# A normalisation border in which the next phase's first chunk runs on unscaled x, with reordered pair ends, in a three-block transformer kernel

## The chip, the core and the metric

One core of a Trainium2 chip. The metric is the time of one execution on the device in microseconds; several runs of one kernel agree within 0.1%. TensorE (PE) does matmuls and loads weights (PEld), VectorE (DVE) and ScalarE (ACT) do elementwise work, GpSimd (POOL) does elementwise work here, SyncE (SP) issues the weight loads.

## The reference, cut to what matters

512 tokens of width 1024, float32, pass three blocks: a gated linear recurrence with stick-breaking attention ("even"), a matrix-memory mixer with gates ("odd"), each followed by a convolutional gated MLP, and a block of dilated attention and latent sparse attention followed by a gated MLP. Every sub-block begins with

```
h   = rmsnorm(x, g) * (1 + scale) + shift      # scale, shift: from the condition vector, one value per channel
mod = silu(c) @ ada_w + ada_b                  # gives shift, scale, gate for each sub-block
x   = x + gate * sub_block(h)
rmsnorm(x, g) = x * rsqrt(mean(x * x, -1) + 1e-6) * g
```

and the output is a last rmsnorm of x. So between two sub-blocks stands a border: the last residual must be in x before the mean of squares of any token is known, and every input of the next matmul carries 1/rms.

## The kernel before, in words

**Layout.** x lies in SBUF with channels on partitions: `X` is 8 tiles (k = 0 to 7) of 128 channels by 512 tokens. Weights come as 302 chunks of 128x1024 float32 in one stream (`wstream`). A chunk of a "tile" phase holds the 8 k tiles for 128 output channels. Products are done in three passes of a rounded format: high x high, high x low, low x high, so each operand is split into a high half (`w_hi`, `h_hi`) and a low half (`w_lo`, `h_lo`). One chunk is 8 x 3 = 24 matmuls of 512 columns into one PSUM bank `gemm0` to `gemm3` (L477 to L479).

**The weight stream.** SyncE loads chunk n into one of 2 raw slots. GpSimd (`split_at`, L432 on) waits until TensorE has finished chunk n-4, does a tiny gate instruction (L439), writes the high half (L440) and subtracts for the low half (L442), into one of 4 slots. `w_split` counts chunks ready, `pe_done` chunks finished.

**Residual phases.** `even_out`, `odd_out` and `attn_out` have 8 chunks of 8 k tiles; `down0` to `down2` have 8 times three chunks with 22 k tiles. Chunk m of the output gives channel tile m. VectorE, when `pe_done` says so, adds gate x bank to `X[m]` (`residual`, L1234); ScalarE squares it (L2085); VectorE adds the square to `sq_acc` (`add_square_prev`, L1511). The last tile is done in two halves (`last_residual`, L1241; squares L2098). VectorE does residual m, then the addition for m, then residual m+1, in this order.

**The border** (`norm`, on each engine). TensorE sums `sq_acc` and the last square over partitions (L581), ScalarE takes the root (L1890), VectorE the reciprocal (L1267), TensorE spreads 1/rms over the partitions (`token_rows`, L608). VectorE then scales tile k (`scaled`, L1281: X x gain x 1/rms), ScalarE adds the shift and rounds (`high_tiles`, L1906), VectorE gives the low half (`low`, L1288), k by k. TensorE fills its waits with matmuls on constants (`keep_warm`, L574). The next phase starts with `first_tiles` (L533, L534, L518): two chunks at once, k by k, as tiles become ready, in an order written by hand; then chunk by chunk. Borders r = 1, 2, 3, 5 stand in front of `ffn0`, `odd_in`, `ffn1` and `ffn2`; "first", "second", "third" and "fourth border" below mean these.

**The odd mixer's pair end.** Heads go in pairs g = 0 to 3. VectorE makes the weights of a head (`mweights`, L1641, L1645), sums them over blocks (`mweight_sum`, L1652 to L1655), copies the inverse norms as a high and low pair (`pair_copy`, L1666, L1667). TensorE multiplies values (`mvalues`, L950), sums squares and denominators (`msums`: L955, L959), spreads inverse norms (`minv_spread`, L983) and starts `odd_out` with three chunks at once, between whose k steps stand `turn_sums` (L989) and other small steps.

**Attention's pairs.** For p = 0 to 7 TensorE turns the exponentials (`turn`, pieces c = 0 to 4, L1156), spreads inverse sums (L1167, piece 5), multiplies values (L1182), and does the scores of pair p+2 (L1133) between pieces 1 and 2. ScalarE does the exponentials (L2307) and copies each turned piece out of PSUM (L2318, L2320, L2325); VectorE adds biases (L1804, L1808), takes maxima with the logits (`logits`, L1821), and normalises the output (L1838, L1842). A piece may be turned only when the copy two pieces back is done.

## Time and profile before

| what | value |
|---|---|
| median of 3 runs | 1936.18 us (1935.46 to 1936.76) |
| the profiled execution | 1939.17 us |
| its span, first to last instruction | 1937.4 us |
| mean granted clock of TensorE | 0.993 |
| busy: PE, DVE, ACT, POOL | 98%, 53%, 23%, 62% |
| chain that ended last | PE 92%, DVE 5%, ACT 2%, DMA 1% |

The chain is the work that ended last, followed back from the end. The granted clock is a share of TensorE's full speed (2.4 GHz); 0.50 is the lower level (1.2 GHz). In a timeline each line gives the start in us from the span's start, the length in us, the engine, the line of the kernel, the operation, output <- inputs, the shape and how many instructions are merged; in brackets stands the idle time of the engine before it and what ended it. A matmul is listed with its full latency (0.39 us) while the next starts 0.23 us after it.

### The profile page before, as it was taken

How to read it: one execution, taken by the hardware profiler on the slowest of the kernel's cores; microseconds unless marked ns; L12 is line 12 of the kernel's file. 1: busy time of each engine (PE TensorE's matmuls, PEld its weight loads, DVE VectorE, ACT ScalarE, POOL GpSimd, SP SyncE). 2: the span in 40 equal slices, each digit the busy share in tenths (PEclk: the TensorE clock that was granted, in tenths of full speed). 3: DMA queues.
4: the chain of work that ended last, by engine and by line, in shares of the span. 5: the costliest groups of instructions: out<-in, count | busy, mean ns of one | idle time of the engine just before them, and what ended most of it. 6: DMA issues, size and time to landing. Idle time of an engine off the chain costs nothing.

```text
span 1937.4 us, 25522 instructions
## 1 busy us (share of the span) xinstructions
PE 1906.3 (98%) x8976; PEld 1541.9 (80%) x8976; DVE 1033.7 (53%) x1518; ACT 441.9 (23%) x774; POOL 1197.1 (62%) x915
## 2 busy tenths in 40 slices
PE   8999999999999999999999999999999999999998
PEld 5888868888888887767888888887776788888887
DVE  4565357666655554586666563243888443232222
ACT  4211342211110022342211111022239221111000
POOL 3844315888777956434688887755551456666673
PEclk9999999999999999999999999999999999999999
DMA  8522223555554432211455553332220122322332
GB/s 339 178 99 95 94 83 109 195 195 195 195 195 176 172 100 83 75 55 55 163 195 195 195 184 120 108 109 87 66 87 1 49 83 97 97 97 97 99 108 76
DMA packets 67665, 242.26 MB, mean 125 GB/s; under 512 B 7658, under 2 KB 8170, under 8 KB 67602
## 3 DMA queue, kind: packets, MB, share of 16 engines
q1 hardware_dynamic: 65536, 237.01, 35.6%
q10 hardware_dynamic: 2066, 4.38, 0.7%
q8 instruction: 44, 0.72, 0.2%
q14 instruction: 19, 0.16, 0.0%
HBM read 239.26 MB, written 2.10 MB: 125 GB/s over the span
## 4 chain that ended last, share of the span: by engine, by line
PE 92%; DVE 5%; ACT 2%; DMA 1%; issue 0%; ACTq 0%; DVEq 0%
PE gemm L477 23%; PE gemm L479 23%; PE gemm L478 23%; PE gemm L533 2%; PE gemm L534 2%; PE gemm L504 2%; PE gemm L505 2%; PE gemm L506 2%; PE gemm L518 2%; PE mix L770 1%; DVE sq_acc L1511 1%; PE gemm L1182 1%; PE mix L608 1%; PE gemm L1156 1%; PE mix L574 1%; PE mix L1133 1%
## 5 line engine op out<-in xcount | busy, mean ns | idle before, releaser
L442 POOL TENSOR_TENSOR w_lo<-w_raw,w_hi 128x1024 fp32r<-128x1024 f32 x302 | 741.5, 2455 | 25.2
L477 PE MATMUL gemm<-h_hi,w_hi 128*128 128x512 f32 x1464 | 571.7, 391 | 0.0
L479 PE MATMUL gemm<-h_hi,w_lo 128*128 128x512 f32 x1464 | 569.8, 389 | 0.0
L478 PE MATMUL gemm<-h_lo,w_hi 128*128 128x512 f32 x1464 | 569.6, 389 | 0.0
L439 POOL TENSOR_TENSOR pool_gate<-pool_gate 128x1 f32<-128x1 f32 x298 | 116.5, 391 | 602.4 <-PE gemm L479 337.6
L440 POOL TENSOR_SCALAR w_hi<-w_raw 128x1024 fp32r<-128x1024 f32 x302 | 341.0, 1129 | 26.8 <-DMA w_raw<-wstream 26.8
L479 PEld LDWEIGHTS gemm<-h_hi,w_lo 128*128 128x128 f32 x1464 | 274.8, 188 | 57.1
L478 PEld LDWEIGHTS gemm<-h_lo,w_hi 128*128 128x128 f32 x1464 | 274.9, 188 | 57.0
L477 PEld LDWEIGHTS gemm<-h_hi,w_hi 128*128 128x128 f32 x1464 | 274.9, 188 | 56.9
L1216 DVE CUSTOM_DVE_ANT_0 ada_raw<-ada_raw,c_act 128x1024 f32<-128x1024 f32 x128 | 224.8, 1772 | 100.4 <-DMA ada_raw<-adastream 100.4
L479 PE MATMUL gemm<-p_hi,w_lo 128*128 128x512 f32 x528 | 205.4, 389 | 0.0
L477 PE MATMUL gemm<-p_hi,w_hi 128*128 128x512 f32 x528 | 205.4, 389 | 0.0
L478 PE MATMUL gemm<-p_lo,w_hi 128*128 128x512 f32 x528 | 205.4, 389 | 0.0
L1234 DVE SCALAR_TENSOR_TENSOR x_res<-gemm,modv,x_res 128x512 f32<-128x512 f32 x42 | 31.4, 747 | 204.8 <-PE gemm L479 190.7
L1539 DVE TENSOR_TENSOR work<-work,gemm 128x512 f32<-128x512 f32 x66 | 45.4, 688 | 177.8 <-PE gemm L479 140.4
L1541 DVE TENSOR_TENSOR p_lo<-work,p_hi 128x512 f32 x66 | 89.9, 1362 | 61.4 <-ACT p_hi L2123 61.4
L1511 DVE TENSOR_TENSOR sq_acc<-sq_acc,sq_tile 128x512 f32<-128x512 f32 x42 | 104.7, 2494 | 29.4 <-ACT sq_tile L2085 29.4
L477 PEld LDWEIGHTS gemm<-p_hi,w_hi 128*128 128x128 f32 x528 | 99.1, 188 | 20.7
L478 PEld LDWEIGHTS gemm<-p_lo,w_hi 128*128 128x128 f32 x528 | 99.1, 188 | 20.6
L479 PEld LDWEIGHTS gemm<-p_hi,w_lo 128*128 128x128 f32 x528 | 99.1, 188 | 20.4
L2085 ACT ACTIVATE sq_tile<-x_res 128x512 f32<-128x512 f32 x42 | 26.6, 633 | 378.0 <-DVE x_res L1234 378.0
L2117 ACT ACTIVATE work<-work 128x512 f32<-128x512 f32 x44 | 27.8, 633 | 308.5 <-DVE work L1534 308.5
(376 smaller groups left out, 2216.5 us busy)
## 6 DMA issues: line engine op xcount, KB each, us to landing
w_raw<-wstream SPq DMA_DIRECT2D x302, 512.0 KB, 3.5
ada_raw<-adastream SPq DMA_DIRECT2D x128, 512.0 KB, 4.3
a_early<-adastream SPq DMA_DIRECT2D x8, 1024.0 KB, 18.6
out<-x_res SPq DMA_DIRECT2D x8, 256.0 KB, 2.2
x_res<-x_in SPq DMA_DIRECT2D x2, 512.0 KB, 5.1
x_res<-x_in ACTq DMA_DIRECT2D x2, 512.0 KB, 7.7
c_act<-c_in ACTq DMA_DIRECT2D x2, 512.0 KB, 5.9
b_dist<-const_in ACTq DMA_DIRECT2D x1, 512.0 KB
```

Source lines behind the costliest of these rows:

```text
L439: pool.tensor_tensor(pgate[:], pgate[:], pgate[:], ALU.mult)
L440: pool.tensor_scalar(whi[s][:], raw[:, u % RAW, :], 1.0, 0.0, ALU.mult, ALU.add).then_inc(w_hi_done, 1)
L442: pool.tensor_tensor(wlo[s][:], raw[:, u % RAW, :], whi[s][:].bitcast(F32), ALU.subtract).then_inc(w_split, 1)
L477: pe.matmul(out_ap, w_h, r_h, start=first, stop=False)
L478: pe.matmul(out_ap, w_h, r_l, start=False, stop=False)
L479: return pe.matmul(out_ap, w_l, r_h, start=False, stop=last)
L504: pe.matmul(G[j][:], a, wh, start=(k == 0), stop=False)
L505: pe.matmul(G[j][:], a, wl, start=False, stop=False)
L1216: dve.tensor_tensor_reduce(w, w, c, 1.0, start, ALU.mult, ALU.add, total).then_inc(ada_used, 1)
L1511: dve.tensor_tensor(sqacc[:], sqacc[:], sqt[:, m % 2, :], ALU.add).then_inc(sq_added, 1)
L1539: dve.tensor_tensor(work[:, 2 + jj, :], y, G[2 * jj + 1][:], ALU.mult).then_inc(gfree[2 * jj + 1], 1)
L1541: dve.tensor_tensor(Plo[:, ds(2 * i + jj, 1), :].rearrange("p a t -> p (a t)"), work[:, 2 + jj, :], Phi[:, ds(2 * i + jj, 1), :].rearrange ...
```

## The change

At borders r = 1, 2, 3, 5 the next phase's chunk 0 is multiplied with u = X x gain, without 1/rms and without the shift. ScalarE makes u's high half for each tile as its residual comes in (ahead of the square), VectorE the low half (`unscaled_low`). VectorE further adds the two halves of chunk 0's weights (`whole_weights`) and forms the products of weights and shift, summed over k (`shift_products`, 8 instructions, each waiting for the one before); TensorE sums these over partitions into one column. TensorE runs chunk 0 between the border's own small matmuls (`norm_beside`), in place of the constant matmuls; VectorE multiplies the full bank by 1/rms and adds the column (`scale_first_chunk`). The normalised tiles are made as before, now without the first tile's halves, and `first_tiles` runs chunks 1 to 3 together.

Apart from the borders: at the odd mixer's pair end the last two weight sums, `gated(6)`, the pair copy, the spreads and the square sums stand in another order. In the attention the last two scores of a pair come between pieces 3 and 4; the logits take their blocks in the order 3, 1, 2, 0; VectorE copies five turned pieces of pairs 6 and 7 in ScalarE's place, and turn 0 of pair 7 stands ahead of the values of pair 6.

```diff
+NEXT = {1: ("ffn0", 1, 24, 32), 2: ("odd_in", 2, 48, 56), 3: ("ffn1", 3, 72, 80), 5: ("ffn2", 6, 120, 128)}
+VECTOR_PIECES = [(6, 2), (6, 3), (6, 4), (7, 1), (7, 3)]
...
@@ TensorE
-            def first_tiles(phase, fill, count=2, before={}):
+            def first_tiles(phase, fill, count=2, before={}, begin=0):
...
-                if done == 0 and phase in FILL:
+                if done == 0 and phase in [nxt[0] for nxt in NEXT.values()]:
+                    first_tiles(phase, FILL[phase], 3, begin=1)
+                    first = 1
+                elif done == 0 and phase in FILL:
...
+            def norm_beside(r):
...
+                pe.wait_ge(w_split, n + 1)
+                pe.wait_ge(gfree[0], G0[phase][0])
+                chunk_tiles((0, 1))
+                pe.wait_ge(sq_added, KT * r + KT - 1)
+                partial_sums(0, sqacc, True, False)
+                pe.wait_ge(sq_ready, KT * (r + 1))
+                partial_sums(0, sqt[:, 1, :], False, True).then_inc(norm_sum, 1)
+                chunk_tiles((2, 3))
+                bc[0] += 1
+                pe.wait_ge(rstd_ready, bc[0])
+                pe.matmul(M[0][:, 0:1], shift_sums, const("ones")[:, 0:1], start=True, stop=True)
+                token_rows(rstdps, 0).then_inc(rstd_bc, 1)
+                chunk_tiles((4, 5, 6, 7)).then_inc(pe_done, 1)
...
@@ TensorE, odd pair end (g == 3), after mvalues(6)
+            pe.wait_ge(sig("msq"), 6)
+            pe.wait_ge(sig("mabs"), 1)
+            msquares(5)
+            mvalues(7)
+            minv_spread(0)
+            minv_spread(1)
+            pe.wait_ge(sig("mwsum"), 7)
+            pe.wait_ge(sig("msq"), 7)
+            msquares(6)
+            mdenominator(6)
+            minv_spread(2)
+            minv_spread(3)
             pe.wait_ge(sig("mnum"), 8)
+            def last_squares():
+                minv_spread(4)
...
+                mdenominator(7)
+                msquares(7)
...
@@ TensorE, attention
-                turn(p, (0, 1))
+                turn(p, (0, 1) if p < 7 else (1,))
                 if p + 2 < 8:
-                    scores(p + 2)
-                turn(p, (2, 3, 4))
+                    scores(p + 2, SCORE_ORDER[:6])
+                turn(p, (2, 3))
+                if p + 2 < 8:
+                    scores(p + 2, SCORE_ORDER[6:])
+                turn(p, (4,))
                 inverse_rows(p)
+                if p == 6:
+                    turn(7, (0,))
                 values(p)
...
@@ VectorE, borders
+            def unscaled_low(r, k):
+                uhi, ulo = unscaled(r)
+                dve.scalar_tensor_tensor(out=ulo[:, k, :], in0=X[:, k, :], scalar=norm_gain(r)[:, k:k + 1], in1=uhi[:, k, :].bitcast(F32),
+                                         op0=ALU.mult, op1=ALU.subtract).then_inc(sig("u_tiles"), 1)
...
+                link(dve.tensor_tensor(both, whi[n % SPL][:].bitcast(F32), wlo[n % SPL][:].bitcast(F32), ALU.add))
...
+                link(dve.tensor_scalar(shift_sums, both[:, 0:P], modv[:, shift:shift + 1], None, ALU.mult))
+                for k in range(1, KT):
+                    link(dve.scalar_tensor_tensor(out=shift_sums, in0=both[:, k * P:(k + 1) * P], scalar=modv[:, shift + k:shift + k + 1],
+                                                  in1=shift_sums, op0=ALU.mult, op1=ALU.add))
...
+            def scale_first_chunk(phase):
+                dve.wait_ge(pe_done, N0[phase] + 1)
+                link(dve.tensor_copy(shift_bias, M[0][:, 0:1]))
+                link(dve.tensor_copy(sqacc[:], rstdps[:]))
+                link(dve.tensor_tensor(G[0][:], G[0][:], sqacc[:], ALU.mult))
+                link(dve.tensor_scalar(G[0][:], G[0][:], shift_bias, None, ALU.add))
...
@@ VectorE, residual_tiles (even_out, odd_out, attn_out)
                     residual(N0[phase] + m, m, m % 4, gate)
                     add_square_prev(r, m)
+                    unscaled_low(r, m)
+                    if m == KT - 4:
+                        whole_weights(r)
+                    if m == KT - 3:
+                        shift_products(r)
                 last_residual(N0[phase] + KT - 1, KT - 1, 3, gate)
...
@@ VectorE, down
+                            if r in NEXT:
+                                unscaled_low(r, 4 * i + m)
+                                if 4 * i + m == KT - 2:
+                                    whole_weights(r)
+                                    shift_products(r)
...
@@ VectorE, odd pair end: mweights(7) first, then
+            pair_copy(GIR, GM[0:EARLY_HEADS, :], EARLY_HEADS)
+            mweight_sum(6)
             normed_head(0)
             normed_head(1)
             split_head(0)
+            mweight_sum(7)
             split_head(1)
             normed_head(2)
+            gated(6)
             normed_head(3)
...
@@ VectorE, attention
+                if p == 7:
+                    copy_piece(7, 1)
+                    copy_piece(7, 3)
                 if p >= 1:
                     pair_low(p - 1)
+                if p == 6:
+                    for c in (2, 3, 4):
+                        copy_piece(6, c)
...
@@ ScalarE, squares
                     act.wait_ge(gfree[m % 4], m // 4 + G0[phase][m % 4] + 1)
+                    if r in NEXT:
+                        act.activation(unscaled(r)[0][:, m, :], X[:, m, :], ACT.Identity, scale=norm_gain(r)[:, m:m + 1])
                     act.wait_ge(sq_added, KT * r + m - 1)
```

## Rows read from the trace of the kernel before

**Rows 1.** The page, part 1: busy time and share of the span of each engine
```profile
PE 1906.3 (98%) x8976; PEld 1541.9 (80%) x8976; DVE 1033.7 (53%) x1518; ACT 441.9 (23%) x774; POOL 1197.1 (62%) x915
```
**Rows 2.** PE's waits (us, times, longest); its timeline (start, us) at attention's end
```profile
PE gemm L1156 <- ACT b_pt L2320: 5.7, 8, 2.0
...
1498.21 1.09 PE L1156 MATMUL gemm<-cst,ada_raw 128*128 128x128 f32 x8
...
1502.86 1.08 PE L1156 MATMUL gemm<-cst,ada_raw 128*128 128x128 f32 x4 [2.02 <-ACT b_pt L2320]
...
1516.25 0.50 PE L533 MATMUL gemm<-h_hi,w_hi 128*128 128x512 f32 x1
```
**Rows 3.** Timeline of PE at the odd mixer's pair end
```profile
869.83 0.73 PE L983 MATMUL mix<-o_gi_hilo,o_sel 40*128 40x512 f32 x2 [2.52 <-DVE o_gi_hilo L1667]
870.48 4.12 PE L950 MATMUL gemm<-o_w,o_v 128*128 128x512 f32 x8
...
881.37 0.44 PE L989 MATMUL mix<-cst,o_gm 40*128 40x40 f32 x4
```
**Rows 4.** Timeline of PE at the first border
```profile
321.68 0.95 PE L581 MATMUL mix<-cst,sq_acc 128*128 128x1 f32 x8
...
327.61 0.47 PE L533 MATMUL gemm<-h_hi,w_hi 128*128 128x512 f32 x1
```
**Rows 5.** Timeline of DVE, then PE, over odd_out and the third border
```profile
896.20 0.75 DVE L1234 SCALAR_TENSOR_TENSOR x_res<-gemm,modv,x_res 128x512 f32<-128x512 f32 x1 [2.56 <-PE gemm L518]
...
900.32 0.74 DVE L1234 SCALAR_TENSOR_TENSOR x_res<-gemm,modv,x_res 128x512 f32<-128x512 f32 x1
...
924.87 0.86 DVE L1241 SCALAR_TENSOR_TENSOR x_res<-gemm,modv,x_res 128x256 f32<-128x256 f32 x2
...
923.13 0.39 PE L478 MATMUL gemm<-h_lo,w_hi 128*128 128x512 f32 x1
923.36 0.39 PE L479 MATMUL gemm<-h_hi,w_lo 128*128 128x512 f32 x1
...
931.01 0.47 PE L533 MATMUL gemm<-h_hi,w_hi 128*128 128x512 f32 x1
```
**Rows 6.** Timeline of DVE at the first border
```profile
317.88 2.83 DVE L1511 TENSOR_TENSOR sq_acc<-sq_acc,sq_tile 128x512 f32<-128x512 f32 x1 [0.70 <-ACT sq_tile L2085]
321.88 0.88 DVE L1241 SCALAR_TENSOR_TENSOR x_res<-gemm,modv,x_res 128x256 f32<-128x256 f32 x2 [1.17 <-PE gemm L479]
```
**Rows 7.** Timeline of POOL at the first border
```profile
317.76 2.40 POOL L442 TENSOR_TENSOR w_lo<-w_raw,w_hi 128x1024 fp32r<-128x1024 f32 x1
```
**Rows 8.** Timeline of all engines, cut to POOL and linked DVE instructions
```profile
752.65 1.21 DVE L1602 TENSOR_TENSOR_SCAN o_gb<-o_gm,o_gf 8x512 f32<-8x512 f32 x1
...
753.82 1.05 POOL L440 TENSOR_SCALAR w_hi<-w_raw 128x1024 fp32r<-128x1024 f32 x1
753.89 1.50 DVE L1603 TENSOR_TENSOR o_ga<-o_gi,o_gb 8x512 f32<-8x512 f32 x1
754.95 2.71 POOL L442 TENSOR_TENSOR w_lo<-w_raw,w_hi 128x1024 fp32r<-128x1024 f32 x1
755.43 3.30 DVE L1605 TENSOR_TENSOR_SCAN o_gm<-o_ga 8x512 f32<-8x512 f32 x1
```
**Rows 9.** A group by line (busy, mean ns), then L1808 and L1227 alone (ns min/median/max)
```profile
L1906 ACT ACTIVATE h_hi<-work,modv 128x512 fp32r<-128x512 f32 x35 | 25.4, 725 | 18.7 <-DVE work L1281 17.9
...
L1808 DVE SCALAR_TENSOR_TENSOR b_bias<-b_dist,b_score x32: 279/483/684, 1463.6 to 1492.8; 128x128 f32<-128x128 f32 x8, 128x256 f32<-128x256 f32 x8, 128x384 f32<-128x384 f32 x8, 128x512 f32<-128x512 f32 x8
...
L1227 DVE TENSOR_TENSOR modv<-mod_sums,cols x32: 161/924/2235, 60.9 to 1171.0; 128x4 f32 x22, 128x4 f32<-128x4 f32 x10
```
**Rows 10.** Timeline of POOL ahead of the second border (down0 to odd_in)
```profile
675.14 2.39 POOL L442 TENSOR_TENSOR w_lo<-w_raw,w_hi 128x1024 fp32r<-128x1024 f32 x1
...
687.09 0.19 POOL L439 TENSOR_TENSOR pool_gate<-pool_gate 128x1 f32<-128x1 f32 x1 [0.48 <-PE gemm L479]
```
**Rows 11.** Stretches: us, PE, PEld, DVE, ACT, POOL busy (x), PEclk, DMA share, GB/s
```profile
1504.00:1508.00 4.00, 4.00 (x24) 2.37 (x26) 0.00 (x0) 1.17 (x2) 0.00 (x0) 0.50 0.01 4
```

More of the change, by code:

```diff
@@ L85, with copies_by_scalar, copies_by_vector @@
 BANK_J = [(1, 384), (2, 0), (1, 0), (0, 0)]
+def copies_by_scalar(p, c):
+    return sum(6 * q + d <= 6 * p + c and (q, d) not in VECTOR_PIECES for q in range(8) for d in range(6))
+def copies_by_vector(p, c):
+    return sum(6 * q + d <= 6 * p + c for q, d in VECTOR_PIECES)
 def slopes():
@@ L1895, in norm @@
                     act.preload_act_table(table)
-                high_tiles(shift)
+                for k in range(KT):
+                    if k == 4:
+                        act.wait_ge(pe_done, N0[NEXT[r][0]] + 1)
+                    act.wait_ge(t_ready, scaled[0] + k + 1)
+                    act.activation(Hhi[:, k, :], work[:, k % 4, :], ACT.Identity, bias=modv[:, shift + k:shift + k + 1]).then_inc(hhi_ready, 1)
+                scaled[0] += KT
+                act.wait_ge(h_ready, KT * (fill + 1))
             def high_tiles(shift):
-                act.wait_ge(t_half, borders[0])
+                act.wait_ge(t_half, 1)
                 act.activation(Hhi[:, 0, 0:HALF], work[:, 0, 0:HALF], ACT.Identity, bias=modv[:, shift:shift + 1])
```

184 lines of the change are left out of this document (123 added, 61 removed).

## The prediction, made before the change was run

> **What bounds the kernel now.** I read the page first. TensorE is busy for 98% of the span [rows 1], so time can only go where it issues something that isn't needed, waits, or runs at its lower clock. The waits of PE add up to little: 5.7 us behind ScalarE's copies of turned weights [rows 2], 2.5 us at the odd mixer's end [rows 3], and 1.3 us at the third border. The rest of what can be had is at the norm borders. At the first, the last useful matmul makes room at 321.68 and the next phase starts at 327.61 [rows 4]: 5.93 us of sums, spread and warming matmuls. The second border and the fourth repeat this within 0.15 us. The third takes 931.01 - 923.59 = 7.42 us (923.36 and one matmul pitch, 923.36 - 923.13 = 0.23) [rows 5], since its last residual is 1.3 us late.
>
> The second thing to see is how VectorE and GpSimd take turns. The addition of squares at 317.88 took 2.83 us, and ended 0.5 us after GpSimd's 317.76 + 2.40 [rows 6, 7]: only the last 0.5 was its own. Residuals, which read PSUM, keep to 0.75 in the same stretches [rows 5]. So a VectorE instruction with two SBUF inputs waits for the GpSimd instruction that runs, and GpSimd waits for it. When both are behind, one chunk's residual, square and addition and one weight split go round in 900.32 - 896.20 = 4.1 us [rows 5]. Three VectorE instructions linked by semaphores show what a chain does while GpSimd has work: L1602 ended, GpSimd's 753.82 took the turn, L1603 stood 1.50 us, GpSimd's 754.95 took the next, and L1605 stood 3.30 us instead of about 1.2 [rows 8]. Even a 128x4 addition costs 0.92 us in the median against 0.16 at least [rows 9].
>
> **The change, part by part.** *Borders, what TensorE does.* One chunk is 24 matmuls, 5.44 us. It moves into the border; warming matmuls go. With nobody late, TensorE needs, from its last matmul: k 0,1 1.36; sums 0.8 and 0.8; k 2,3 1.36; the shift column and four row spreads 1.15 (12 records took 1.34, so 8 take 0.9, and 0.25 for the column); k 4 to 7 2.72: 8.2 us. Before, border and chunk were 5.93 + 5.44 = 11.37. That is 3.2 us saved a border, and the most there is. The square root (0.26) and reciprocal lie under k 2,3. ScalarE's new wait for this chunk ahead of tile 4 costs nothing, tile 4 being due 3 us after it is done even then; no DMA is moved, and SyncE's weight loads wait for splits as before. Afterwards three chunks share each k step, 9 x 0.227 = 2.04 us, against VectorE's 1.32 a step, so by k = 6 it is 4.3 us ahead, which covers the four instructions on the full bank (about 2.3 us by four instructions like the 0.6 to 0.75 ones; 2.3 us a border if the cover were gone). GpSimd's next splits come one at a time, 3.6 us each, under 5.44: nothing.
>
> *Borders, what VectorE and ScalarE get.* For each of seven residuals ScalarE gets one more activation, ahead of the square (0.72, 0.62 after overlap) [rows 9]: the addition is ready 2.07 us after the residual instead of 1.45, which GpSimd's 2.40 hides. VectorE gets a subtraction with two SBUF inputs, 0.6: the round grows from 4.1 to 4.7. Against 5.44 a chunk it still catches up, by 0.74 instead of 1.34. Once come the sum of the weight halves and eight linked products of 128 columns: such an instruction takes 0.28 for 128 columns and 0.68 for 512 [rows 9], so the sum over 1024 takes 1.2, a product 0.28, 0.31 with the link, all eight 2.5 us if nothing came between. They stand ahead of residual 6, and that ahead of the last one, so whatever they wait, the norm waits.
>
> *First border, step by step.* The pair was done six chunks before the last, at 321.67 - 32.7 = 289.0. Residual 4 starts at 289.1 + 4 x 4.7 = 307.9; its addition ends 311.7, the subtraction 312.35. GpSimd's waiting first half-split takes the turn to 313.4, the weight sum runs to 314.5, GpSimd's second to 316.85, addition 5 to 317.35, subtraction to 318.0. Then GpSimd to 319.1, product 1, GpSimd to 321.6, product 2. TensorE's last matmul at 321.67 has freed another slot, so GpSimd goes again, to 323.0 and, after product 3, to 325.5; products 4 to 8 end at 327.0. Residual 6, two activations, addition at 329.1, subtraction, and the last residual starts at 330.2, not 321.88 [rows 6]. From there: squares 1.45, sums 0.8, 1.36, 1.15, 2.72 = 7.5, so the three chunks start at 337.7. Before, the same point was 327.61 + 5.44 = 333.05: **+4.6 us**. TensorE stands from 323.0 to 329.7 meanwhile. The fourth border has the same rhythm: **+4.6**.
>
> *Third border.* Three chunks finish together at 896, so the round of 4.7 never catches up: the last residual starts at about 937.3 instead of 924.87 [rows 5], the three chunks at 944.7 against 931.01 + 5.44 = 936.45: **+8.2**.
>
> *Second border.* A chunk of down0 takes 15 us and nobody is late, but the weight sum waits for the split that ends at 677.5 [rows 10], and the eight products then meet three more splits, the last released by the last matmul (687.09 [rows 10]). By the same walk they end at 691.2 and the last residual is 4.2 us late: **+0.5**. Two turns fewer and it is -3.2; I take +0.5, because the last two products fall on that last split.
>
> *The clock.* After a wait of 2.02 us the attention's end ran at a granted 0.50, the lower of the two levels (1.2 GHz) [rows 2, 11], until its values ended at about 1509, some 6.6 us. Waits of 6 us and more at each of three borders should do the same. Bounds: nothing, to half of 6.6, 3.3 each; I take 2 each, since part of the work there waits for others anyway: **+6**. The Trainium skill (TensorE: Matmul & The Clock Gate, "Why this matters for your kernels") warns against letting TensorE stand between bursts; by that rule all three borders lose, as in this term, and taking out the warming matmuls is wrong wherever something else is late.
>
> *Odd pair end.* TensorE's wait of 2.5 us and the eight matmuls that took 4.12 us, at half clock [rows 3, 11], instead of 2.3, come from VectorE's weight sum and pair copy ahead of them. Putting both behind the last weights lets the last values run at 867.5 instead of 870.48; what is put off returns as waits of 0.4, 0.2 and 1.3 us (a spread that needs the third normed head). I get 879.4 for what stood at 881.37 [rows 3]: **-2** (0 to -4).
>
> *Attention.* Six of the eight waits for a copy are short: 5.7 less 2.02 and some 1.7 leaves 0.34 us each [rows 2]; two scores put there fill it, but ScalarE's copy can come only 0.1 to 0.3 earlier: five pairs, -1.2. At the end 1498.21 to 1516.25 is 18.0 us [rows 2]; with VectorE copying five pieces (0.69 each, like its other reads of a bank) turn 4 of pair 6 starts at 1501.2, not 1502.86, its values at 1503.4 at full clock, and the last values end at 1511.9: -4.3. Together **-5.5** (-2 to -8).
>
> **Sum.** 4.6 + 0.5 + 8.2 + 4.6 + 6 - 2 - 5.5 = +16.4 us. The profiled execution took 1939.17 us (span 1937.4), 3.0 above the median of 1936.18, so the sum is put on the median: 1952.6.
>
> **The rivals.** *Chain in one piece.* The products go through without GpSimd between them. The Trainium skill (VectorE: DVE Perf Modes, "The DRAIN you can't avoid") reports that semaphores between VectorE instructions cost nothing extra; by that rule the chain is as long linked as not. The mechanism here: 2.5 us in one stretch. The last residual is then 3.5 us late at borders one and four (-0.3 each), on time at the second (-3.2), 8.5 late at the third (+3.4, and 2 of clock): +1.6 - 7.5, 1930. The linked three [rows 8] speak against it, with three instructions out of three giving way; four unlinked ones were not all interrupted.
> *No holding at all.* The new instructions overlap GpSimd. The borders reach 8.2 us, only the third keeps 0.5 of lateness: -9.1 - 7.5 = -16.6, 1919.6. Subtractions of the same form stood 2 us behind GpSimd elsewhere, so this needs a trace wrong about three kinds of instruction; a luckier order of splits would come near it.
> *Pair ends bring nothing.* The waits move to the third head's spread and the copies; the borders as forecast: 1960.
> The sign turns on where the last residual starts: late by less than about 4 us, a border gains; by more, it loses.
>
> **How the numbers follow.** Forecast 0.66 (own range 1942 to 1962: the clock term from 0 to 10, the second border from -3.2, the ends from -3 to -11), one piece 0.17, no holding 0.12, no gain at the ends 0.05. The range 1928 to 1961 leaves out no holding and the top of the last. About 0.2% (3.9 us) is what a measurement can tell from none. Faster: no holding and most of one piece, 0.26; same, the rest of it and the forecast's lowest edge, 0.08; slower 0.66.
>
> **What would show it.** In the changed kernel's timeline: GpSimd's half-splits between the products at borders one, three and four; products at 0.28 with stands of 1.1 and 2.4 among them; the last residual 8 us (third border: 13) after the phase's last matmul; a wait of PE for the addition of squares of 6 to 12 us in three places, and a granted clock of 0.50 after it. At the two pair ends, a continuous PE. I am wrong if those residuals start within 1 us, or if the chunk beside the norm is done before the root.

## The result, and the profile after

The changed kernel took **1968.9 us** in the median of four runs (1965.12 to 1973.89) beside 1936.47 for the kernel before: a ratio of **1.016, interval 1.0144 to 1.0177**. Slower, as forecast, but above the range of 1928 to 1961. The profiled execution was the fastest of the four, 1965.12 us with a span of 1963.2; that of before, 1939.17, was longer than all four of its runs. So the two traces are 26.0 us apart where the medians are 32.4; the accounts below are made between the traces, and what separates them from the medians comes up with the experiments. One execution of experiment 10 was in a slow state (2736 us at a granted clock of 0.65) and is left out of its ratio.

First the page, part 1, and then the largest waits of PE (us in total, times, longest) of the changed kernel:

```profile
PE 1904.3 (97%) x8920; PEld 1539.6 (78%) x8920; DVE 1098.5 (56%) x1603; ACT 456.2 (23%) x797; POOL 1220.6 (62%) x915
```

```profile
PE mix L608 <- DVE sq_acc L1657: 23.7, 3, 11.3
PE mix L608 <- ACT sq_tile L2282: 6.4, 1, 6.4
...
PE gemm L500 <- DVE work L1680: 2.5, 2, 1.3
...
PE gemm L1229 <- ACT b_pt L2505: 1.5, 1, 1.5
```

Beside [rows 1], TensorE has 56 instructions fewer and is busy for 2 us less, yet the span grew by 26. The first two rows are the four borders: 30.1 us of waits where there was 1.3. The last row is the attention's end, 1.5 us instead of the 5.7 of [rows 2].

VectorE at the first border, with the columns start, us, engine, line, operation, tiles; a bracket is the idle time ahead and what ended it. Then GpSimd in the same stretch, then TensorE:

```profile
312.14 2.06 DVE L1368 TENSOR_TENSOR work<-w_hi,w_lo 128x1024 f32<-128x1024 f32 x1
...
317.59 1.07 DVE L1373 TENSOR_SCALAR work<-work,modv 128x128 f32<-128x128 f32 x1
318.70 7.68 DVE L1375 SCALAR_TENSOR_TENSOR work<-work,modv 128x128 f32<-128x128 f32 x7
326.42 0.75 DVE L1314 SCALAR_TENSOR_TENSOR x_res<-gemm,modv,x_res 128x512 f32<-128x512 f32 x1
...
329.75 0.87 DVE L1321 SCALAR_TENSOR_TENSOR x_res<-gemm,modv,x_res 128x256 f32<-128x256 f32 x2
```

```profile
318.66 2.39 POOL L465 TENSOR_TENSOR w_lo<-w_raw,w_hi 128x1024 fp32r<-128x1024 f32 x1
321.80 0.22 POOL L462 TENSOR_TENSOR pool_gate<-pool_gate 128x1 f32<-128x1 f32 x1 [0.75 <-PE gemm L502]
321.99 1.05 POOL L463 TENSOR_SCALAR w_hi<-w_raw 128x1024 fp32r<-128x1024 f32 x1
323.12 2.34 POOL L465 TENSOR_TENSOR w_lo<-w_raw,w_hi 128x1024 fp32r<-128x1024 f32 x1
```

```profile
321.26 0.39 PE L502 MATMUL gemm<-h_hi,w_lo 128*128 128x512 f32 x1
...
329.22 1.87 PE L608 MATMUL mix<-cst,sq_acc 128*128 128x1 f32 x8 [6.21 <-DVE sq_acc L1657]
...
331.12 1.87 PE L608 MATMUL mix<-cst,sq_tile 128*128 128x1 f32 x8
332.85 0.77 PE L500 MATMUL gemm<-p_hi,w_hi 128*128 128x512 f32 x1
...
340.29 0.39 PE L556 MATMUL gemm<-h_hi,w_hi 128*128 128x512 f32 x1
```

The seven products of L1375 took 7.68 us. One by one their durations are 2.50, 0.35, 0.35, 1.17, 2.40, 0.35 and 0.35: each long one ends within 0.15 us after a GpSimd instruction (318.66 + 2.39, 321.99 + 1.05, 323.12 + 2.34), and where GpSimd stands a product takes 0.35. The last residual starts at 329.75, 8.3 us after the phase's last matmul (321.26 and one pitch, 321.49), and the three chunks start at 340.29.

Then the clock. Stretches of the changed kernel: from and to, length, busy time of PE, PEld, DVE, ACT, POOL, then PEclk:

```profile
322.00:327.00 5.00, 1.01 (x5) 0.51 (x3) 4.85 (x5) 0.00 (x0) 3.38 (x3) 1.00 0.67 220
328.00:337.00 9.00, 7.75 (x29) 7.08 (x30) 2.96 (x6) 3.35 (x6) 0.00 (x0) 0.50 0.19 79
338.00:341.00 3.00, 3.00 (x15) 2.45 (x14) 2.87 (x5) 1.68 (x3) 0.46 (x2) 1.00 0.00 0
700.00:709.00 9.00, 4.70 (x16) 4.12 (x17) 4.51 (x7) 2.91 (x5) 1.97 (x1) 0.50 0.44 144
942.00:958.00 16.00, 9.07 (x34) 8.31 (x35) 7.99 (x14) 4.15 (x7) 2.34 (x1) 0.50 0.35 129
1584.00:1593.00 9.00, 6.19 (x22) 5.62 (x23) 3.68 (x7) 4.15 (x7) 0.00 (x0) 0.50 0.18 60
```

TensorE had stood since 322.85 when the clock fell at about 327, and it did not come back until after the sums, two k steps and most of the spread: all four borders run the first half of their critical matmuls at 1.2 GHz, and k 4 to 7 again at 2.4 GHz. Eight sums take 1.87 us instead of 0.95 [rows 4].

An account of the two traces, by landmarks of TensorE. A border is the time from the phase's last matmul to the next phase's three chunks (before: its start plus one chunk of 5.44 us):

| stretch | before | after | difference | forecast |
|---|---|---|---|---|
| border 1 | 11.37 | 18.80 | +7.4 | +4.6 and 2 of clock |
| ffn0 | 234.04 | 235.49 | +1.45 | 0 |
| border 2 | 11.51 | 17.28 | +5.8 | +0.5 |
| odd mixer to its last matmul | 225.31 | 223.12 | -2.2 | -2 |
| border 3 | 12.86 | 24.64 | +11.8 | +8.2 and 2 |
| index and attention phases | 217.80 | 212.76 | -5.0 | -5.5 |
| border 4 | 11.38 | 18.06 | +6.7 | +4.6 and 2 |

The sum is 25.9, for spans 25.8 apart. Two differences are not in the table, since they cancel. ffn1 took 1.5 us more, as ffn0 did. And at the border ahead of the index phase (r = 4), which the change leaves alone, the kernel before took 8.3 us from the last matmul to the next phase (1290.17 to 1298.44) and the changed kernel 6.8 (1315.90 to 1322.69): before's trace has a granted clock of 0.50 there from 1294.0 to 1297.5, the other has 1.00. Six of the fourteen traces of this case have that stretch (before and experiments 5 to 8 and 10), so it is not the change that takes it away, and it hides ffn1's loss.

### The profile page after: what moved, and what is told of

It reads as the page before. It is cut to its first block, busy times and chain, and to the rows that moved or that the text cites. A ratio compares the mean times of both kernels' runs of the same rounds, so it can differ in the third digit from the quotient of the medians.

```text
span 1963.2 us, 25500 instructions
## 1 busy us (share of the span) xinstructions
PE 1904.3 (97%) x8920; PEld 1539.6 (78%) x8920; DVE 1098.5 (56%) x1603; ACT 456.2 (23%) x797; POOL 1220.6 (62%) x915
## 4 chain that ended last, share of the span: by engine, by line
PE 75%; issue 8%; DVE 6%; POOL 6%; DMA 3%; ACT 1%; SPq 0%; POOLq 0%; DVEq 0%; ACTq 0%
PE gemm L500 19%; PE gemm L502 19%; PE gemm L501 19%; POOL w_lo L465 3%; POOL w_hi L463 2%; DMA w_raw<-wstream 2%; PE gemm L527 2%; PE gemm L528 2%; PE gemm L529 2%; PE mix L828 1%; DVE work L1375 1%; PE gemm L1257 1%; PE gemm L1229 1%; PE mix L1199 1%; PE mix L500 1%
## 5 line engine op out<-in xcount | busy, mean ns | idle before, releaser
L500 PE MATMUL gemm<-h_hi,w_hi 128*128 128x512 f32 x1408 | 551.1, 391 | 2.6 <-DVE work L1680 2.5
L502 PE MATMUL gemm<-h_hi,w_lo 128*128 128x512 f32 x1408 | 548.5, 390 | 0.0
L501 PE MATMUL gemm<-h_lo,w_hi 128*128 128x512 f32 x1408 | 548.4, 389 | 0.0
L463 POOL TENSOR_SCALAR w_hi<-w_raw 128x1024 fp32r<-128x1024 f32 x302 | 361.6, 1197 | 26.8 <-DMA w_raw<-wstream 26.8
L500 PE MATMUL gemm<-p_hi,w_hi 128*128 128x512 f32 x552 | 217.3, 394 | 0.0
L501 PE MATMUL gemm<-p_lo,w_hi 128*128 128x512 f32 x552 | 216.4, 392 | 0.0
L502 PE MATMUL gemm<-p_hi,w_lo 128*128 128x512 f32 x552 | 216.4, 392 | 0.0
L1687 DVE TENSOR_TENSOR p_lo<-work,p_hi 128x512 f32 x66 | 104.8, 1588 | 61.4 <-ACT p_hi L2309 61.4
L1657 DVE TENSOR_TENSOR sq_acc<-sq_acc,sq_tile 128x512 f32<-128x512 f32 x42 | 80.2, 1909 | 46.6 <-ACT sq_tile L2269 46.6
L2309 ACT ACTIVATE p_hi<-work 128x512 f32 x66 | 41.7, 632 | 155.2 <-DVE work L1685 155.2
## 6 DMA issues: line engine op xcount, KB each, us to landing
a_early<-adastream SPq DMA_DIRECT2D x8, 1024.0 KB, 18.6
```

The source lines that it names most:

```text
L463: pool.tensor_scalar(whi[s][:], raw[:, u % RAW, :], 1.0, 0.0, ALU.mult, ALU.add).then_inc(w_hi_done, 1)
L500: pe.matmul(out_ap, w_h, r_h, start=first, stop=False)
L501: pe.matmul(out_ap, w_h, r_l, start=False, stop=False)
L502: return pe.matmul(out_ap, w_l, r_h, start=False, stop=last)
L1657: dve.tensor_tensor(sqacc[:], sqacc[:], sqt[:, m % 2, :], ALU.add).then_inc(sq_added, 1)
L1687: dve.tensor_tensor(Plo[:, ds(2 * i + jj, 1), :].rearrange("p a t -> p (a t)"), work[:, 2 + jj, :], Phi[:, ds(2 * i + jj, 1), :].rearrange ...
```

## The experiments

Twelve kernels ran, each beside the kernel before on the same chip. Over all these runs the kernel before had a median of 1938.4 us (1935.18 to 1945.36, 35 runs). That is a spread of 0.5%, where three runs had given 0.1%: a difference of 1 or 2 us between two medians is not resolved here.

**1. The pair ends alone.** The kernel before with the new odd pair end and the new attention, no border work.

```diff
 for g in range(4):
     mweights(2 * g)
-    mweight_sum(2 * g)
+    if g < 3:
+        mweight_sum(2 * g)
...
-            scores(p + 2)
-        turn(p, (2, 3, 4))
+            scores(p + 2, SCORE_ORDER[:6])
+        turn(p, (2, 3))
+        if p + 2 < 8:
+            scores(p + 2, SCORE_ORDER[6:])
+        turn(p, (4,))
```

> The kernel before with the two pair ends of the change and none of its border work. Theory (the parts add up): by the landmarks of the two traces the odd mixer from the second border to the third is 3.96 - 1.82 = 2.1 us shorter with the change and the attention phase 5.0 us shorter, so 1936.5 - 7.1 = 1929.4 us, 1928 to 1931. Rival (the ends gain only because the borders ahead of them left GpSimd less behind): the same ends give less than 3 us here, 1934 or more.

Measured: 1933.85 us, ratio 0.998 (0.997 to 0.9991), 4.1 us less than its kernel before, between theory and rival. Its trace, of an execution of 1936.66 us and so above that median, gives a reason. The odd mixer's last matmul comes 2.6 us earlier and the attention phase is 5.1 us shorter, both as the theory has it. But from the third border's last matmul to the next phase's start it took 10.7 us (923.99 to 934.70) instead of 7.4 [rows 5]. Stretches of this run, and of the kernel with the attention part alone (experiment 12), where nothing ahead of the third border is changed:

```profile
926.40:933.00 6.60, 6.60 (x26) 6.06 (x26) 0.67 (x3) 2.23 (x4) 2.34 (x1) 0.50 0.84 304
```

```profile
925.60:932.20 6.60, 6.60 (x26) 6.06 (x27) 0.82 (x3) 2.25 (x5) 2.50 (x2) 0.50 0.82 289
```

The old third border has a 1.3 us wait, and in some runs half clock follows it, at 3.3 us (in experiment 11 for 3.5 us only, at 1.5), and in some not (the kernel before). With one trace for each kernel, that this is chance and not the changed code is argued, not shown.

**2. The borders alone.** The kernel before with the border work, old ends.

```diff
-            norm(1, 2, col("norm_ffn_g", 0, 8), (24, 32))
+            norm_beside(1, 2)
...
+                    if m == KT - 4:
+                        whole_weights(r)
+                    if m == KT - 3:
+                        shift_products(r)
```

> The kernel before with the border work alone, old pair ends. Theory: the borders and what follows them carry the whole loss, 7.4 + 5.7 + 11.8 + 6.7 at the four borders and 1.5 in the first feed-forward, 33 us by the landmarks of the traces: 1969 to 1976 us, last residual 8 us after the phase's last matmul at borders one and four, 7 at two, 13 at three. Rival (the new pair end puts the third border's VectorE behind, so a part of that loss belongs to the ends): the third border costs 5 us less here than the 11.8 of the change, 1964 or less.

Measured: 1974.88 us, ratio 1.0182 (1.016 to 1.0203), 37 us more than before. The borders took 19.6, 17.7, 24.2 and 18.7 us; the third cost 11.3 more than before's 12.86, so the rival, that the ends had a part in it, falls. The parts add up: -4.1 and +36.9 make +32.8, the whole change +32.4.

**3. Warming matmuls in the waits, first size.**

```diff
                 chunk_tiles((0, 1))
+                keep_warm({1: 54, 2: 2, 3: 96, 5: 54}[r])
                 pe.wait_ge(sq_added, KT * r + KT - 1)
                 partial_sums(0, sqacc, True, False)
+                keep_warm({1: 2, 2: 48, 3: 2, 5: 2}[r])
```

> The changed kernel with warming matmuls put into the time in which TensorE waits at the four borders, nothing else altered. Theory (the low clock is a cost of its own of 2.4 to 3.8 us a border, 11.6 in all: from the last residual to the three chunks it took 10.5, 10.0, 11.3 and 9.9 us against 7.5 worked out at full clock): no stretch at 0.50 at the borders, sums of 0.95 us for eight instead of 1.87, and 1968.9 - 11 = 1958 us, 1955 to 1961. Rival (the stretch behind the last residual is set by VectorE and ScalarE, the clock costs what was forecast or less): 1963 or more.

Measured: 2036.54 us, ratio 1.051 (1.0484 to 1.0536), far outside both ranges. The theory was not at fault but the size: I had taken one warming matmul as a single pass.

```profile
324.24 23.47 PE L601 MATMUL mix<-cst 128*128 128x256 f32 x108
...
347.54 0.95 PE L608 MATMUL mix<-cst,sq_acc 128*128 128x1 f32 x8
```

That is TensorE at the first border: 54 warming matmuls are 108 records of 0.217 us, 23.5 us where 6 were to be filled. But the sums that follow take 0.95. The kernel served to size the next.

**5. The same, sized: 13, 12, 26 and 13 matmuls in the long wait of each border, one in the short.**

```diff
+                keep_warm({1: 13, 2: 1, 3: 26, 5: 13}[r])
...
+                keep_warm({1: 1, 2: 12, 3: 1, 5: 1}[r])
```

> The changed kernel with warming matmuls in the waits of the four borders, now sized by the last run (54 of them took 23.5 us, 0.43 each): 13, 13, 26 and 13 of them for waits of 6.2, 6.4, 11.3 and 6.2 us. Theory (the lower clock costs 2.4 to 3.8 us a border): no stretch at 0.50 at the borders, the sums 0.95 us for eight, and 11 us less than the changed kernel's 1968.9, so 1958 us, 1955 to 1961. Rival (VectorE and ScalarE set the pace there, the clock costs what was forecast, 6 us, or less): 1963 or more.

Measured: 1958.83 us, ratio 1.0095 (1.0067 to 1.0123), 10 us less than the changed kernel: the theory's number. TensorE at the fourth border:

```profile
1580.18 5.77 PE L601 MATMUL mix<-cst 128*128 128x256 f32 x26
1586.63 1.05 PE L608 MATMUL mix<-cst,sq_acc 128*128 128x1 f32 x8 [0.67 <-DVE sq_acc L1659]
...
1588.52 1.05 PE L608 MATMUL mix<-cst,sq_tile 128*128 128x1 f32 x8 [0.30 <-ACT sq_tile L2284]
```

From the last residual to the three chunks it took 7.65 us at borders two and four (705.78 to 713.43, 1587.15 to 1594.80), against 10.0 and 9.9 in the changed kernel; 7.5 was the forecast's. At borders one and three it still was 9.2 and 9.3: short waits were left everywhere, and there a spell at 0.50 followed (335.3 to 338.7 at the first). Between the two traces the four borders are 7.8 us shorter, together. What remains is 20 us over the kernel before, with the lateness as it was: 8.3, 7.2, 13.4 and 8.3 us.

**4. The shift column on TensorE.** No weight sum and no products on VectorE; the same column from 16 one-column matmuls.

```diff
+                for k in range(KT):
+                    for w in (whi, wlo):
+                        pe.matmul(M[0][:, 0:1], w[s][:, k * P:(k + 1) * P].bitcast(F32), modv[:, shift + k:shift + k + 1],
+                                  start=(k == 0 and w is whi), stop=(k == KT - 1 and w is wlo))
...
-                    if m == KT - 4:
-                        whole_weights(r)
-                    if m == KT - 3:
-                        shift_products(r)
```

> The changed kernel without the weight sum and the eight linked products on VectorE: the column of shifts comes from 16 matmuls of one column (the high and the low half of the weights times the shift), put ahead of the sum of squares. Theory (those nine instructions, each giving GpSimd a turn, make the last residual late): it starts within 1 us of the phase's last matmul at borders one, two and four, and 5 to 6 us after it at the third, where the rounds of 4.6 us still do not catch up; 16 matmuls cost 1.9 us at 0.12 each; a border takes 9.9 us instead of 11.4, the third 13 to 16, so 1936.5 - 4.5 + 2 + 1.5 - 7.1 = 1928 us, 1925 to 1932. Rival A (the subtraction beside each residual is what makes it late): last residuals 4 us late and more at all borders, above 1945. Rival B (the small matmuls cost more than 0.2 us each on TensorE's path): lateness gone but 1933 to 1938.

Measured: 1951.19 us, ratio 1.0056 (1.0037 to 1.0075). The lateness is gone as the theory says: last residuals 0.20, 0.20, 5.0 and 0.20 us after the phase's last matmul. The subtraction of rival A is cleared, but for the 5.0 us of the third border. But the borders took 16.6, 15.0, 16.6 and 16.6 us, not 9.9, and rival B was too small as well. TensorE at the first border, and two stretches of it:

```profile
330.91 0.57 PE L651 MATMUL mix<-modv,w_hi 128*128 128x1 f32 x2
...
332.62 1.84 PE L608 MATMUL mix<-cst,sq_acc 128*128 128x1 f32 x8
334.33 1.85 PE L608 MATMUL mix<-cst,sq_tile 128*128 128x1 f32 x8
336.04 0.77 PE L500 MATMUL gemm<-p_hi,w_hi 128*128 128x512 f32 x1
```

```profile
326.96:330.80 3.84, 3.84 (x30) 3.61 (x29) 0.94 (x3) 1.36 (x3) 3.45 (x3) 1.00 0.80 273
331.00:341.00 10.00, 10.00 (x41) 9.32 (x41) 1.13 (x3) 1.55 (x2) 0.00 (x0) 0.50 0.30 106
```

Each of the 16 is two records, 0.22 us together, so 3.6 us at full clock. And though TensorE waited for nothing, its clock fell at 331, 2.6 us into the one-column matmuls, and the sums and k steps behind them ran at half: 4.3 us of column, 3.4 of sums. At the third and fourth border it fell at the same place; at the second the column ran at full clock (701.61 to 705.09) and the clock fell at 706.4, in the sums behind it. An engine can be busy for 100% of a stretch and still lose its clock, as here at all four borders.

**6. Two products instead of eight.**

```diff
-                link(dve.tensor_scalar(shift_sums, both[:, 0:P], modv[:, shift:shift + 1], None, ALU.mult))
-                for k in range(1, KT):
-                    link(dve.scalar_tensor_tensor(...))
+                whole = both.rearrange("p (k t) -> p k t", k=KT)
+                link(dve.tensor_tensor(whole, whole, modv[:, shift:shift + KT].unsqueeze(2).broadcast_to([P, KT, P]), ALU.mult))
+                link(dve.tensor_reduce(shift_sums, both.rearrange("p (k t) -> p t k", k=KT), axis=mybir.AxisListType.X, op=ALU.add))
```

> The changed kernel with the eight linked products as two instructions, one product over 1024 columns and one sum over the eight pieces. Theory (what costs is that each instruction waits for GpSimd's half-split in progress; fewer instructions, fewer stands): the two end 1.5 to 2 us earlier than the eight at each border, 1968.9 - 7 = 1962 us, 1959 to 1965. Rival (the length of the chain's own work is what counts, 2.6 us against 3.1): 1965 to 1969. A sum over strided pieces that takes over 3 us by itself would make it slower than 1969.

Measured: 1950.3 us, ratio 1.0058 (1.0036 to 1.0081), 18.6 us less than the eight: the theory's side, at more than twice its size. VectorE at the first border, then at the second:

```profile
318.19 2.06 DVE L1374 TENSOR_TENSOR work<-work,modv 128x1024 f32<-128x1024 f32 x1
320.29 2.04 DVE L1375 TENSOR_REDUCE work<-work 128x128 f32<-128x1024 f32 x1
322.36 0.75 DVE L1314 SCALAR_TENSOR_TENSOR x_res<-gemm,modv,x_res 128x512 f32<-128x512 f32 x1
...
327.24 0.86 DVE L1321 SCALAR_TENSOR_TENSOR x_res<-gemm,modv,x_res 128x256 f32<-128x256 f32 x2
```

```profile
688.13 1.23 DVE L1368 TENSOR_TENSOR work<-w_hi,w_lo 128x1024 f32<-128x1024 f32 x1 [3.57 <-POOL w_lo L465]
689.40 1.95 DVE L1374 TENSOR_TENSOR work<-work,modv 128x1024 f32<-128x1024 f32 x1
691.38 2.02 DVE L1375 TENSOR_REDUCE work<-work 128x128 f32<-128x1024 f32 x1
694.03 0.88 DVE L1321 SCALAR_TENSOR_TENSOR x_res<-gemm,modv,x_res 128x256 f32<-128x256 f32 x2 [0.63 <-PE gemm L502]
```

Two instructions of the same content take 4.1 us where eight took 8.8. The product stands once for GpSimd; the sum, with a single SBUF input, runs beside GpSimd's half-split (319.26 to 322.51) and takes no turn at all. At the second border they are done at 693.4, just before the phase's last matmul (693.77) frees the next slot: VectorE waits for TensorE again, the last residual is 0.3 us late, the border is 8.4 us instead of 17.3, and its clock is not lost. At the others the last residual is still 5.2, 10.3 and 5.2 us late. Borders: 16.0, 8.4, 20.4 and 15.0, together 19.0 us less. I had priced two turns, and neither the clock nor the turn that the last matmul releases. The Trainium skill (SBUF — State Buffer, "SBUF: two separate sides") calls the port pair of VectorE and GpSimd an exclusive lock, held for a whole instruction by whichever starts first; the rows of both kernels agree: the products' stands end where GpSimd's instruction ends.

**7. No products.** The nine instructions are left out and with them the first chunk's shift; the rest is the changed kernel.

> The changed kernel with the weight sum and the eight products left out (the first chunk's shift is missing from the output). Theory (they alone make the last residual late, and the 8.2 us of a border stand as worked out): last residual 0.2 us after the phase's last matmul at borders one, two and four, 5 at the third; 8.2 us from last matmul to the three chunks instead of 11.4, at the third 13 to 16 with its clock; 1938 - 9.6 + 3 + 1.5 - 4 (the pair ends as measured) = 1929 us, 1926 to 1932. Rival (the clock falls in any case once the warming matmuls are gone, since one-column matmuls do not hold it): 10.5 to 11 us at borders one, two and four, 1935 to 1938, and stretches at 0.50 at all four.

Measured: 1931.82 us, ratio 0.9961 (0.9948 to 0.9974), in the range. A stretch that is the whole first border:

```profile
321.76:330.16 8.40, 8.40 (x51) 7.41 (x50) 4.36 (x9) 4.29 (x7) 3.57 (x3) 1.00 0.70 248
```

TensorE never waits, the clock stays at 1.00 and the border takes 8.4 us, 0.2 over the 8.2 worked out. Borders two and four take 8.4 too. So the warming matmuls were not missed where nobody was late. The third took 15.6, with its residual 5.0 late and 6.8 us at 0.50. Against the changed kernel it is 37 us, the price of nine instructions at each of four borders, which take 4.0 us a border when nothing is in their way (1.2 for the sum, 8 x 0.35).

**8. The products later.** The weight sum behind the last residual, the products spread over the k steps of the three chunks, the column's matmul at the step k = 5. Nothing left out.

```diff
+                whole_weights(r)
+                products = iter(range(KT))
                 rms_n[0] += 1
                 ready(inverse_rms(4, rms_n[0]))
...
                 for k in range(KT):
+                    for _ in range((0, 1, 2, 2, 2, 1, 0, 0)[k]):
+                        shift_product(r, next(products))
```

> The changed kernel with its weight sum put behind the last residual and the eight products into the first k steps of the next phase's other three chunks, where VectorE has about 0.7 us a step to spare and GpSimd has no slot to fill; the column's matmul waits until the fifth step. Nothing is left out. Theory (same work, moved off the chain that sets the norm): the borders as without the products, plus 1 to 2 us at each where the weight sum meets a half-split ahead of the reciprocal: 1931 us, 1928 to 1936. Rival (VectorE loses its lead of 4.3 us in the three chunks and TensorE waits there for low tiles): waits of PE for h_lo of 2 us and more at each border, 1938 to 1945.

Measured: 1939.29 us, ratio 1.0003 (0.9992 to 1.0013): no difference from before. The time is in the rival's range (1938 to 1945) and above the theory's; the wait is another than the rival's, for the column and for banks and not for low tiles. The borders took 8.2, 8.2, 15.9 and 8.2 us. What they gained was asked back behind them. TensorE waited three times for the column (3.1 us together), ffn0 took 237.5 us instead of 234.0, and the odd mixer to its last matmul 226.4 where the changed kernel took 223.1: VectorE's lead was spent and it came late to the first groups of both.

**9. A version meant to beat both.** Late products at three borders, the column and the scaling a step later, the third border as before, both new ends.

```diff
-NEXT = {1: ("ffn0", 1, 24, 32), 2: ("odd_in", 2, 48, 56), 3: ("ffn1", 3, 72, 80), 5: ("ffn2", 6, 120, 128)}
+NEXT = {1: ("ffn0", 1, 24, 32), 2: ("odd_in", 2, 48, 56), 5: ("ffn2", 6, 120, 128)}
...
-                    if k == KT - 2:
+                    if k == KT - 1:
                         scale_first_chunk(phase)
```

> A version meant to beat both: the late products at borders one, two and four, their column and the scaling one k step later, the third border as in the kernel before, and both new pair ends. Theory: 8.2 to 8.4 us from last matmul to the three chunks at the three borders (-3.1 each), 1.5 us lost again at the start of ffn0, the pair ends as measured (-4): 1938.3 - 9.3 + 1.5 - 4 = 1926.5 us, 1924 to 1930. Rival (VectorE has no lead left in the three chunks, so what the border saves is waited for there and in the first groups of the feed-forward): 1932 or more.

Measured: 1932.69 us, ratio 0.9974 (0.9964 to 0.9984): faster than the kernel before by 5 us, of which the ends alone bring 4. The rival is right. The three borders took 8.19 us each, 9.7 less together, and TensorE then waits in ffn0, and in odd_in (the last line, from its list of waits):

```profile
344.94 0.38 PE L579 MATMUL mix<-cst,n_tail 128*128 128x1 f32 x2 [0.40 <-DVE n_tail L1395]
352.56 0.80 PE L510 MATMUL gemm<-h_hi,w_hi 128*128 128x512 f32 x1 [2.33 <-DVE work L1703]
...
PE gemm L510 <- DVE o_qk L1761: 2.7, 1, 2.7
```

ffn0 took 239.1 us, 5.0 more than before, and the odd mixer to its last matmul 228.1, where experiment 1 with the same pair end took 222.7: 5.3 more, all of it ahead of the gates in odd_in. In both places 3.4 us at 0.50 follow the wait (352.5 to 355.9, 721.1 to 724.6). ffn2 gave back 0.8. That is 11.1 us for the 9.7 gained. VectorE's work on the first groups (L1703 and L1761 here) stands behind the products, the scaling and, in ffn0, the modulation sums, so a bank comes free late.

**10. The same with a hold at the third border.**

```diff
+                if r == 3:
+                    keep_warm(3)
                 pe.wait_ge(sq_added, KT * r + KT - 1)
```

> The same kernel with three warming matmuls (1.3 us) ahead of the third border's sums, where TensorE waits 1.2 us. Theory (with the new pair end the wait at the third border is followed by 6.8 us at 0.50, which took 3.3 us of the pair ends' gain in the run with the pair ends alone): no stretch at 0.50 there and 2 to 3 us less than the same kernel without them. Rival (that stretch comes from the run, not from the wait): no difference within 0.1%.

Measured: 1933.57 us, ratio 0.9975 (0.9962 to 0.9989): no difference from the same kernel without the hold. But it tests neither side. In the profiled run of experiment 9 the last residual of the third border starts 0.2 us after the last matmul and not 1.3, TensorE doesn't wait there at all, and the border takes 5.9 us without a low stretch; with the hold it takes 7.2, the 1.3 of the hold itself.

**11 and 12. Each end alone.**

> The kernel before with the odd mixer's new pair end alone. Theory: 2.6 us gained by the third border's last matmul, as in the run with both ends, and given back by a third border that runs at 0.50: 1938.3, 1937 to 1940. Rival (the low stretch there was a matter of that one run): 1936 or less.

> The kernel before with the attention part alone. Theory: the attention phase 5.1 us shorter, 1938.3 - 5.1 = 1933.2, 1932 to 1935, with its waits for ScalarE's copies down from 5.7 us to under 2 and no stretch at 0.50 at its end. Rival (the stretch at 0.50 made half of the old end's length and may come back): 1935 or more.

Measured: the odd end 1937.99 us, ratio 0.9999 (0.9989 to 1.0009); the attention part 1937.15, 0.9997 (0.9987 to 1.0007). The first is what its theory says, though its own trace gives back 1.5 of the 2.6 us and not all. The second is not: a median 1.2 us lower where 5.1 were expected. Nor do the two add up to experiment 1: 0.4 and 1.2 us here, 4.1 there, with an interval of about 2 us on each; how much the ends bring over runs is known no better than that. The traces give two reasons for the second. One is the third border's stretch at 0.50, shown above. The other is the old end. In the profiled run of experiment 11, which has the old attention, that phase took 214.7 us and not 217.8. A stretch of its end, and one of the kernel before:

```profile
1480.00:1510.43 30.43, 26.59 (x230) 18.39 (x226) 17.80 (x60) 24.35 (x63) 5.23 (x4) 1.00 0.00 1
```

```profile
1502.60:1508.80 6.20, 5.94 (x30) 3.60 (x32) 0.00 (x0) 1.79 (x4) 0.00 (x0) 0.50 0.01 3
```

The same wait of 2.0 us was followed by half clock in one run and not in the other. The new end saves 2.0 us against a run of the first kind and 5.1 against one of the second.

## Why the prediction was wrong

**What held.** The direction, and the mechanism down to the rows. The last residual was forecast 8.5, 13.7 and 8.5 us after the last matmul at borders one, three and four (330.2, 937.3); it came at 8.3, 13.4 and 8.2. The products stood for GpSimd's half-splits as the three linked instructions of [rows 8] had. With them gone the lateness was 0.2 us (5.0 at the third border), and the border 8.4 for a forecast 8.2. The odd mixer gave 2.2 to 2.6 us for 2. The rivals "chain in one piece" and "no holding at all" fell with the rows; "pair ends bring nothing" falls by experiment 1 (interval 0.997 to 0.9991), but neither end alone is told from nothing. The first of them had a rule of the Trainium skill beside it (VectorE: DVE Perf Modes, "The DRAIN you can't avoid"), that semaphores between VectorE instructions cost nothing extra. The trace agrees with it as far as it goes: 0.35 us and a start-to-start of 0.39 where GpSimd stands. It says nothing of a neighbour that takes the turn.

**What failed: sizes of four terms.** In the order of their weight:

1. *The clock, +6.* I took 2 us at each of three borders, under the 3.3 of the old attention's end, arguing that part of the work there waits for others anyway. It doesn't: behind the last residual stands a chain of TensorE's own, two sets of sums, two k steps, the spread, and only 0.3 to 0.7 us of it waits. The low stretches lasted 10.2, 10.2, 17.1 and 10.2 us. Against the 7.65 of experiment 5 from the last residual to the three chunks, the four borders took 10.5, 10.0, 11.25 and 9.9: 2.9, 2.35, 3.6 and 2.2, **11.0 us for 6**, the second border among them. Removing it by the sized warming gave 10 between medians, and 7.8 at the borders of its trace, where two borders kept a spell at 0.50. With the Trainium skill's warning of bursts (TensorE: Matmul & The Clock Gate, "Why this matters for your kernels") the trace agrees in sign; taking out the warming matmuls is harmless where nobody is late, at 8.4 us with a clock of 1.00, and costs this much where somebody is.
2. *The second border, +0.5.* It cost 5.8. I had the weight sum start at 677.5, 9.2 us ahead of the last matmul, by the old order of splits [rows 10]. GpSimd in the changed kernel:

```profile
687.60 2.39 POOL L465 TENSOR_TENSOR w_lo<-w_raw,w_hi 128x1024 fp32r<-128x1024 f32 x1
689.94 0.19 POOL L462 TENSOR_TENSOR pool_gate<-pool_gate 128x1 f32<-128x1 f32 x1
690.10 2.07 POOL L463 TENSOR_SCALAR w_hi<-w_raw 128x1024 fp32r<-128x1024 f32 x1
```

The split it waits for ended at 689.99, 5.6 us ahead of the last matmul (695.64), not 9.2. GpSimd was 3.6 us behind its old place and had no gap left between its splits, and six of the eight products stood for one. I had let the new instructions slow VectorE and not GpSimd, which makes the split that they wait for. It wasn't the products that held GpSimd back: in experiments 4 and 7, which have none, the same split ends 5.7 us ahead of the last matmul too, and in experiment 1, which has no border work, 9.5. What is left are the added subtractions and ScalarE's added activations, which no run tried alone. The last residual was 7.3 us late for 4.2, 3.1 of the 5.3 that were missing; the rest is the low clock of point 1.
3. *The pair ends, -7.5.* In the two traces they gave 7.2; over runs 4.1. Of the attention's -4.3 a part was half clock that one execution had [rows 11], and others hadn't. So it is with the odd end, where before's trace has 0.50 from 870.7 to 874.2 ([rows 11], which the prediction names for it, show the attention's end alone): after the same wait of 2.52 us [rows 3] the old end's eight matmuls took 2.42 us in experiment 2 and not 4.12, its odd mixer took 224.6 us and not 225.3, and the new end's 223.1 is 1.5 less. The old third border loses 3.3 us to the same thing in some. I read a stretch that comes and goes as if it stood in every run. The traces are 26.0 us apart and the medians 32.4; these stretches are the part of that difference that I can name. A further one, near 125 us, stood in five of the twelve traces and in neither of the first two; what follows came 3 to 5 us later there.
4. *Costing edits at nothing.* ffn0 and ffn1 each got a wait of 1.2 to 1.3 us for VectorE's second tap (L1680), 1.45 and 1.5 in all; ffn1's is hidden between the traces by the half clock that before's had at the border r = 4. I had named the lead of 4.3 us that covers the scaling, but the cover ends at the three chunks and the first taps stand behind it.

Together: 16.4 + 5.0 (clock) + 3.1 (lateness at the second border) + 1.5 (ffn0) = 26.0, what lies between the traces; 3.4 more for the ends over runs makes 29.4 of 32.4. Half of the last 3 us may be ffn1's 1.5, in the runs of the kernel before that keep their clock at r = 4. The rest I can't place: there is no profile of the changed kernel's longer runs. More clock is a candidate: in experiment 2's trace, the longest of its four runs, the first border stood at 0.50 for 13.8 us and not 10.2, and took 19.6 us for 18.8.

**What stays open.** Whether the low stretches near 125 us, at the border r = 4, at the old third border and at the two old ends have a cause beyond the run was not tried; experiment 10 was meant for one of them and met no wait. Nor was a kernel tried that puts VectorE's work on the first groups of ffn0 and odd_in ahead of the rest, which by experiment 9 is where the borders' gain was lost again.

## What to carry to other kernels

Before work is given to an engine with slack, look at who shares its turn: nine VectorE instructions of 4 us, at four borders, cost 37 us here, since five or six of the nine waited for a GpSimd instruction and they stood ahead of a residual that the norm waits for. Fewer and longer instructions lose less (18.6 us by making eight into two), and work whose result is due 10 us later belongs behind the chain, not in it, if the engine has time left there (experiments 8 and 9: it hadn't). When a wait of TensorE's grows from under 2 us to over 5 ahead of its own serial work, price the half clock on all of that work; and take a term that rests on a clock stretch of one profile as a range, not as a value.

## What the runs showed of the hardware

- TensorE's clock fell to 0.50 at 331.0 in experiment 4 without a wait, 2.6 us into an unbroken run of one-column matmuls at 100% busy (4.8 us at its second border, 701.61 to 706.4); the same border with 16 sums between wide matmuls kept 1.00 (experiment 7).
- A 32-bit matmul of 256 columns is two records of 0.217 us, one of a single column two of 0.11: sixteen of one column cost 3.6 us at full clock.
- Waits of 1.3, 2.0 and 2.5 us were followed by half clock in some executions and not in others, with the same code at that place, at a price of up to 3.3 us (so was the border r = 4, without a wait, at 1.5); the eight of 6 us and more at the borders of the changed kernel and of experiment 2 always were.
- A VectorE sum over eight pieces 128 columns apart (128x1024 in, 128x128 out) took 2.02 to 2.04 us while GpSimd's half-split ran, where products with two SBUF inputs stood.
